# A hybrid sequence block on one core: half 0's convolution norm moved into half 1's state projection, and loads, squares and powers moved at the start of mixing

## The reference, cut to what matters

```python
h = rms_norm(x, g_pre_mix) * (1.0 + sc_m) + sh_m          # 2048 tokens x 1024
z = h @ w_in                                              # value, gate, ssm: 3 x 512 channels
a_out = conv_module(z_val * sigmoid(z_gate), ...)         # 31 taps per channel, layer norm, silu
b_out = s5_layer(z_ssm, ...)                              # complex linear recurrence, gelu, gated by its own projection
mixed = concatenate([rms_norm(a_out, g_out_conv), rms_norm(b_out, g_out_ssm)])
x = x + gt_m * rms_norm(mixed @ w_out, g_post_mix)
h = rms_norm(x, g_pre_ffn) * (1.0 + sc_f) + sh_f
y = moe_ffn(h, ...)                                       # sigmoid router, 8 of 64 experts, shared expert
x = x + gt_f * rms_norm(y, g_post_ffn)
```

## Time and profile before

| what | value |
|---|---|
| three runs | 2805.59, 2814.50, 2821.21 us; median 2814.5 us |
| the profiled execution | 2798.67 us, its span 2797.0 us |
| mean granted TensorE clock of the profiled execution | 0.958 of full speed |
| TensorE busy | 2543.7 us, 91% of the span |
| VectorE, ScalarE, GpSimd busy | 1552.1 us (55%), 1153.4 us (41%), 1384.4 us (49%) |

### The profile page before, as it was taken

The page is one execution under the profiler, slowest core; times in us unless marked ns, Lnnn a source line. Parts: engine busy times, 40 slices in busy tenths (PEclk is TensorE's granted clock), DMA queues, the critical chain, the costliest instruction groups (busy, mean ns, idle before and its releaser), DMA issues.

```text
span 2797.0 us, 49346 instructions
## 1 busy us (share of the span) xinstructions
PE 2543.7 (91%) x11232; PEld 1855.5 (66%) x11233; DVE 1552.1 (55%) x2764; ACT 1153.4 (41%) x1546; POOL 1384.4 (49%) x1726
## 2 busy tenths in 40 slices
PE   4999999957899998899999999999999999999990
PEld 1754664513456666688787877777887878777770
DVE  6379957993676776334333433444445544454535
ACT  5132313324233222344444444445555555555532
POOL 2011206013566665355555555565676677767662
PEclk7999999988899999999999999999999999999995
DMA  8152605454322322877777777788888988888978
GB/s 276 64 98 91 215 6 84 166 200 148 135 98 94 103 91 100 256 194 182 211 194 207 195 197 200 208 229 257 260 259 257 292 266 263 258 264 254 269 213 291
DMA packets 304953, 534.61 MB, mean 191 GB/s; under 512 B 38597, under 2 KB 204485, under 8 KB 304120
## 3 DMA queue, kind: packets, MB, share of 16 engines
q1 hardware_dynamic: 250248, 352.77, 38.0%
q0 software_dynamic: 51472, 173.70, 25.9%
q10 hardware_dynamic: 3168, 7.34, 0.7%
HBM read 395.75 MB, written 138.00 MB: 191 GB/s over the span
## 4 chain that ended last, share of the span: by engine, by line
PE 39%; issue 16%; POOL 8%; POOLq 6%; DVE 2%; DMA 1%; ACT 0%; SPq 0%; another core or an unknown queue 0%; ACTq 0%; DVEq 0%
PE psm L1122 29%; PE psm L1068 5%; PE psm L1115 3%; POOL arena L2265 2%; POOL arena L2262 2%; POOL st L2255 2%; POOLq L2261 1%; POOLq L2283 1%; POOLq L2274 1%; POOLq L2282 1%; POOL arena L2275 1%; PE psm L1090 1%; PE psm L1144 1%; POOL acc_d L2279 1%; DVE arena L2108 1%
## 5 line engine op out<-in xcount | busy, mean ns | idle before, releaser
L1122 PE MATMUL psm<-whi,xhi 128*128 (+1 forms) x1424 | 575.6, 404 | 42.5 <-issue 31.6
L1122 PE MATMUL psm<-whi,xlo 128*128 (+1 forms) x1424 | 559.4, 393 | 0.0
L1122 PE MATMUL psm<-wlo,xhi 128*128 (+1 forms) x1424 | 558.5, 392 | 0.0
L2009 DVE TENSOR_TENSOR arena<-psm,arena 128x256 f32<-128x256 f32 x178 | 75.5, 424 | 618.0 <-ACT arena L1504 612.7
L1122 PEld LDWEIGHTS psm<-whi,xhi 128*128 128x128 f32 x1424 | 269.5, 189 | 115.6 <-issue 65.0
L2270 POOL TENSOR_TENSOR wlo<-raw,whi (+1 forms) x64 | 331.0, 5172 | 20.3 <-ACT whi L1536 20.3
L1504 ACT ACTIVATE arena<-psm 128x256 f32<-128x256 f32 x178 | 68.2, 383 | 588.4 <-PE psm L1122 588.4
L1122 PE MATMUL psm<-whi,hhi 128*128 (+1 forms) x712 | 295.9, 416 | 14.3 <-POOL wlo L2270 7.0
L1122 PEld LDWEIGHTS psm<-whi,xlo 128*128 128x128 f32 x1424 | 269.2, 189 | 57.6
L2279 POOL DMA_INDIRECT acc_d<-arena x162 | 276.8, 1709 | 57.7 <-issue 53.7
L1122 PEld LDWEIGHTS psm<-wlo,xhi 128*128 128x128 f32 x1424 | 269.8, 189 | 50.9
(11 more groups left out here) (379 smaller groups left out, 4016.4 us busy)
## 6 DMA issues: line engine op xcount, KB each, us to landing
raw<-in_we_gate_dram SPq DMA_DIRECT2D x64, 1024.0 KB
raw<-in_we_up_dram SPq DMA_DIRECT2D x64, 1024.0 KB
raw<-in_we_down_dram SPq DMA_DIRECT2D x64, 1024.0 KB
arena<-in_w_ada_dram SPq DMA_DIRECT2D x12, 2048.0 KB
arena<-in_x_dram SPq DMA_DIRECT2D x32, 512.0 KB, 5.4
h_d<-arena SPq DMA_DIRECT2D x17, 512.0 KB, 2.7
arena<-in_w_in_dram SPq DMA_DIRECT2D x16, 512.0 KB, 6.2
mix_d<-bo SPq DMA_DIRECT2D x32, 256.0 KB, 2.3
```

The lines of the kernel that those rows point to most:

```text
L1122: m = TE.matmul(o, a, w, start=(n == 0), stop=(n == len(todo) - 1))
```

## The change

Five edits. Half 0's norm turns 0 to 3 are moved on TensorE, ScalarE and GpSimd behind the last four steps of half 1's `z_ssm` (`NORM_ZS` = 4), turns 4 and 5 to the products `V` of state groups 0 and 1 (`NORM_ZC` = 6), and turns 6 to 9 stay behind `zc` units 0 to 3; `tpk` and `sgk` follow. VectorE takes statistics 0 to 3 ahead of `states(1)`, and 4 to 7 among its groups. In SyncE's queue half 1's loads of the convolution weights q = 2 and of the Toeplitz table (`load_toe`) go behind six of the norm's stores, and q = 3 behind all eight. Four of the seven row loads go up into the stretch behind the last modulation weights; the router bias goes behind the last stores. `squares_joined(0)` and `ssn(0)` stand ahead of the products of the rows, and `rr(0)` ahead of GpSimd's index tables.

```diff
             if h == 0:
                 tpk += [("hT", 0, g, k) for g, k in UNITS]
+            for i in range(NORM_ZS if h else 0):
+                tpk += [("LF", 0, i)]
+                tpk += [("LB", 0, i - 2)] if i >= 2 else []
             tpk += [("UT", h, n) for n in range(8)]
...
+            sgk += [("ln", 0, i - 2) for i in range(2, NORM_ZC if h else 0)]
             for u, (q, b, w) in enumerate(ZC_UNITS):
                 sgk += [("zc", h, q, b)] if w else []
-                sgk += [("ln", 0, u - 2)] if h == 1 and 2 <= u < TPH + 2 else []
+                sgk += [("ln", 0, u + NORM_ZC - 2)] if h and u + NORM_ZC < TPH + 2 else []
...
             load_wz_conv(1, 1)
-            load_toe(1)
-            load_wz_conv(1, 2)
             for i in range(6):
                 store_bo(("ln", 0, i))
-            load_wz_conv(1, 3)
+            load_wz_conv(1, 2)
+            load_toe(1)
             for i in range(6, TPH):
                 store_bo(("ln", 0, i))
+            load_wz_conv(1, 3)
...
                 store_mod(n - 4)
+            for o in (s_mod_out0, s_mod_out1):
+                sp.wait_ge(o, 32)
+            sp.wait_ge(s_h2z_out, 32)
+            for dst, src in ((row[0], mod_d[2]), (rtmp[:, 0], A["g_post_mix"][0]), (rtmp[:, 1], A["g_pre_ffn"][0]),
+                             (rtmp[:, 2], A["g_post_ffn"][0])):
+                SY.dma_start(dst, src.partition_broadcast(P)).then_inc(s_row_in, 16)
...
-            for dst, src in ((row[0], mod_d[2]), (row[1], mod_d[4]), (row[2], mod_d[3]), (row[3], mod_d[5]),
-                             (rtmp[:, 0], A["g_post_mix"][0]), (rtmp[:, 1], A["g_pre_ffn"][0]), (rtmp[:, 2], A["g_post_ffn"][0])):
+            for dst, src in ((row[1], mod_d[4]), (row[2], mod_d[3]), (row[3], mod_d[5])):
                 SY.dma_start(dst, src.partition_broadcast(P)).then_inc(s_row_in, 16)
-            SY.dma_start(wr, A["w_router"][0].rearrange("(k p) e -> p k e", p=P)).then_inc(s_wr_in, 16)
-            SY.dma_start(rbias, A["b_router"][0].partition_broadcast(P)).then_inc(s_wr_in, 16)
             for i in range(3, 5):
                 store_bo(("ln", 1, i))
+            SY.dma_start(wr, A["w_router"][0].rearrange("(k p) e -> p k e", p=P)).then_inc(s_wr_in, 16)
...
@@ TensorE and ScalarE, z_ssm @@
+                    if h and j >= CH - NORM_ZS:
+                        norm_turn(0, j - (CH - NORM_ZS))
@@ TensorE, z_conv @@
                 for n in range(2):
                     input_state(h, n)
+                    if h:
+                        norm_turn(0, NORM_ZS + n)
...
-                    if h == 1 and u < TPH + 2:
-                        norm_turn(0, u)
+                    if h == 1 and u + NORM_ZC < TPH + 2:
+                        norm_turn(0, u + NORM_ZC)
@@ VectorE, states @@
                 if h:
+                    for k in range(NORM_ZS):
+                        norm_stats(k)
                     dve.wait_ge(s_tab_in, 32)
...
-                    if h and n >= 2:
-                        norm_stats(2 * n - 3)
+                    if h and n == 1:
+                        norm_stats(5)
...
-                    if h and 1 <= n <= 3:
-                        norm_stats(2 * n - 2)
-                if h:
-                    for k in range(5, TPH):
-                        norm_stats(k)
+                    if h and n < 3:
+                        norm_stats((4, 6, 7)[n])
@@ GpSimd, gate @@
+                for i in range(NORM_ZC if h else 0):
+                    norm_turn(0, i)
```

More of the change, by code:

```diff
@@ L59 @@
 NADA = 4
+NORM_ZS = 4
+NORM_ZC = 6
 EPS = 1e-6
@@ L369, in build @@
                 tpk += [("hT", 0, g, k) for g, k in UNITS]
+            for i in range(NORM_ZS if h else 0):
+                tpk += [("LF", 0, i)]
+                tpk += [("LB", 0, i - 2)] if i >= 2 else []
             tpk += [("UT", h, n) for n in range(8)]
-            if h == 1:
-                for i in range(TPH + 2):
-                    tpk += [("LF", 0, i)] if i < TPH else []
-                    tpk += [("LB", 0, i - 2)] if i >= 2 else []
+            for i in range(NORM_ZS, TPH + 2 if h else 0):
+                tpk += [("LF", 0, i)] if i < TPH else []
+                tpk += [("LB", 0, i - 2)] if i >= 2 else []
             if h == 0:
@@ L1085, in route @@
                 pe.wait_ge(s_ssn_ready, min(i + 2, NT))
+                if i == 0:
+                    pe.wait_ge(s_wr_in, 32)
                 if i:
@@ L1362, in z_conv @@
                     row_stats(2, xjunk)
+                for i in range(NORM_ZS, NORM_ZC if h else 0):
+                    norm_turn(0, i)
                 for u, (q, b, w) in enumerate(ZC_UNITS):
@@ L2040, in _ @@
             ssn(0)
+            dve.wait_ge(s_row_in, 7 * 16)
+            dve.wait_ge(s_dv_full, DVN["ada", 11] + 1)
+            do(tt(row[0], row[0], rtmp[:, 0], ALU.mult), stt(row[1], row[1], 1.0, rtmp[:, 1], ALU.add, ALU.mult),
+               tt(row[3], row[3], rtmp[:, 2], ALU.mult), V.memset(selcum[:, 0, :], 0.0), V.memset(ones64, 1.0))
+            V.tensor_copy(ndt[:, 3:4], ndt[:, 0:1]).then_inc(s_row_ready, 1)
             for i in range(NT):
@@ L2207, in _, with rr @@
                 norm_turn(1, i)
+            def rr(i):
+                c0 = 16 * (i % 2)
+                pool.wait_ge(s_ssn_ready, i + 1)
+                do(PO.tensor_tensor(st[:, c0 + 2:c0 + 3], st[:, c0:c0 + 1], mhalf[:, :], ALU.pow))
+                PO.tensor_tensor(st[:, c0 + 3:c0 + 4], st[:, c0 + 1:c0 + 2], mhalf[:, :], ALU.pow).then_inc(s_rr_ready, 1)
+            rr(0)
             pool.wait_ge(s_row_ready, 1)
```

18 lines of the change are left out of this document (4 added, 14 removed).

## The result

The changed kernel takes 2789.55 us (median of 20 runs, 2774.21 to 2807.64), the kernel before 2809.34 (20 runs beside it, 2793.08 to 2821.21). The ratio is 0.9937, 95% interval 0.9917 to 0.9958, a gain of 17.7 us (12 to 23); the two medians differ by 19.8, which lies in the same interval. The prediction was 2790 with a gain of 24.7: the direction and both places were right, both were sized too large. That the time itself was met is luck: over 20 runs the median before is 2809.3, and not the 2814.5 of the first three, from which the 24.7 were subtracted.

What follows compares the result with a forecast made beforehand. Bound taken: first `V`, states, statistics 4 to 7, convolution, then GpSimd's store wait ending half 1's norm. Gains 16.9 + 7.8 = 24.7 us took the 2814.5 median to 2789.8, rounded to 2790; range 2780 to 2806.

Steps and rivals of the forecast that it cites:

- both places: Half 0's norm, moved among projection steps and states: 16.9 us gain; start of mixing, at half 1's norm end: 7.8 us.
- The bound: Up to the convolution: first `V`, states, statistics 4 to 7, convolution; 17.8 us between states and convolution, mostly waiting for norm turns.
- First `V`: VectorE's first state operation moves from 396.41 to 400.0, behind added TensorE and ScalarE norm work: 3.6 us loss, bounds 1.8 and 6.
- The states: VectorE's state groups keep 59.0 us, GpSimd doing about the same beside them, some 18 us; bounds 54.5 and 62.
- The convolution: VectorE's convolution falls from 155.7 to 153.0 us as norm products leave its first quarter: gain 2.7, bounds 0 and 4.8.
- Second place: Start of mixing: earlier store of tile 3 lets GpSimd's product 5 start at 662.7, not 670.56; 7.8 us, bounds 0 and 10.9.
- the prediction's own sign: At the end of half 1's norm: the start-of-mixing forecast is wrong if GpSimd still waits for a store.
- 1: Before the convolution: gates of q = 0 replace the norm's statistics as the wait; convolution starts about 467, time 2798; chance 0.14.
- 5: Before `conv(1)`: the change does not do what it says; reduced to 1, with no chance of its own.
- 2: End of half 1's norm: store of tile 4 or 5 late behind `ws_raw` loads, only half 0's norm pays; 2798; chance 0.11.
- 3: SyncE's queue: moved row loads delay segment 8's store and half 1's norm turns; 2800 to 2810 us; chance 0.11.
- 4: TensorE becomes the bound, new waits at `UT` and turns 6 and 9 dropping its clock; 2835 us with 60 delay; chance 0.04.

Runs made afterwards that it cites:

- norm part alone: Only the diff's norm turns, statistics, `yn`, their stores and loads, against the kernel before; rows, first squares and powers unmoved: 2794.68 us, ratio 0.9943.
- rows late: Against the changed kernel, SyncE issues the store of half 1's output tile 3 ahead of the three row loads; no whole time or ratio given.
- `LB` 1 late: Against the changed kernel, second projection of half 0's tile 1, its ScalarE copy and sigmoid moved behind the eight `UT` transposes; ratio 0.9927 to the kernel before.

## Why the prediction was right, and where its sizes were off

**The bound.** Right: the convolution waited for half 0's statistics, and nothing took that wait's place. The norm part alone brings c 12.4 us nearer to z.

**First `V`.** 3.6 us of loss forecast, 1.8 on TensorE and 2.7 less 0.9 on ScalarE; 3.8 measured, of which `LB` 1 is 1.6 and TensorE's longer steps 2.2.

**The states: the mis-sized term.** "GpSimd does about the same beside them" and "I keep 59.0" failed: 62.4, so 3.4 us too few. Even the count was short (18 us of busy time; it is 25.24, since six norm products and two gates lie there, not four and one). And busy time was the wrong measure. A VectorE operation that reads from SBUF alone loses about 0.9 us (0.7 to 1.1 over these traces) to each GpSimd product of two SBUF tensors and 0.3 to 0.5 to a scaling, and one that reads PSUM loses nothing. By that rule on the timelines: four products before, eight after, 4 x 0.9 = 3.6 us, and one scaling fewer at 0.46; measured are 3.5.

The Trainium skill (SBUF — State Buffer, "SBUF: two separate sides") says that the pair of ports is locked by a VectorE operation "in a 2-port perf mode, or with two SBUF inputs (only against a GpSimd op that reads SBUF)" or by the GpSimd operation, and that the other one waits. I had used its lock for all busy time and set it aside for being twice the measured rate. Read with the condition on the operands it agrees with the traces: products fallen beside PSUM readers were free, and beside SBUF readers both sides lengthen (1.74 for 1.26 on GpSimd, 0.88 on VectorE). The passes with one tensor operand that lost too would come under its first clause; no run shows in which mode they ran. For the scaling the traces differ from it: 2.1 us long, it cost 0.3 to 0.5.

**The convolution.** 2.7 us of gain forecast, 2.0 measured. Before, 15 products and one scaling lay in it, after 14 products, which is 1.4 by the count. Added up over its instructions VectorE lost 14.4 us there before and 12.5 after. The rate of the earlier trace rows gave about the right size here because nearly all that GpSimd did there were products.

**Second place.** 7.8 us forecast, 4.25 measured. The forecast had product 5 at 33.8 us behind c; it started at 36.5. Of these 2.7 us, 1.4 are TensorE's slower start behind c in this profile; the forecast had assumed the rhythm of the kernel before: 3.64 us for sixteen matmuls that took 2.98, and 4.53 for eight (644.97) that took 3.60, so that product 5's sigmoid ended 35.0 us behind c and not 33.6. It also made the store's issue 1.1 late. The other 1.3 are the store: it took 7.9 us, not the 5.1 worked out from the loads' mean rate. That this term failed, the store's landing behind three row loads, doesn't hang on one profile: in all seven kernels that issue the store directly behind three row loads product 5 started 7.9 to 8.3 us behind its issue, also where TensorE's start was quick. Product 6 added 1.0, lengthened by a row product of VectorE, which I had costed as hidden ("run while TensorE works"). The same pair, with GpSimd as the one that waits. The kernel with rows late took out both, and its profile had the quick start that the forecast assumed: c to M became 40.6, against 40.8 forecast. By the prediction's own sign ("in the second if GpSimd still waits for a store") this place was half wrong: the wait is 1.70 us, and 3.2 to 3.4 in four other profiles with this order.

**The sum.** 16.9 became 12.5 and 7.8 became 4.25, together 16.8 of 24.7; z to J shows 17.0 and the ratio 17.7 (12 to 23). Two slips in the recorded sums move nothing: by the lock the sum would have been 27.5, not 27.6, and half of 1.07 is 0.54, not 0.58.

**Rivals.** 1 and 5: the gates were 6.1 us early. 2: products 6 and 7 were not held by stores in the changed kernel. 3: the four row loads were issued from 614.9 to 616.6, ahead of c; half 1's first norm turns follow each other at 4.66 us as before (they start 1.0 later behind c, which is TensorE's clock). 4: the granted clock in the convolution was 0.95, before 0.88.

## What to carry to other kernels

When work on GpSimd is moved beside VectorE, count its operations with two SBUF tensors against VectorE's operations that read from SBUF alone, and price each pair by one measured portion (0.9 us for 128x512 here), not by busy time; where VectorE reads PSUM they are free, so the place of a product inside a group is worth as much as its number. A store that frees a buffer goes out ahead of broadcast loads that nobody waits for yet: by bytes and a mean rate its landing is forecast too early. In a kernel whose executions spread by 1%, read a change as distances between two fixed instructions, take TensorE's start behind an idle time out of the comparison (here by the distance to the first product behind it), and let the medians confirm the sum.

## What the runs showed of the hardware that was not expected

The loss of VectorE comes in portions: eight scans of 128x128 take 3.12 us alone, 4.00 beside one GpSimd product and 4.85 beside two. Where GpSimd starts second, it pays: its product took 2.29 us for 1.27 beside a VectorE operation of 128x1024 (1.22 us) that had started 0.05 us before it. A scaling of 128x512 by GpSimd with one tensor and two values for each partition took 2.09 beside PSUM readers and 3.03 beside scans, which lost only 0.3. A store behind three broadcast loads in one queue let its product start 7.9 to 8.3 us after its issue, in seven kernels; without them directly in front it was 5.8 in the kernel before and with the norm part alone, and at most 6.0 with rows late. Behind idle times of 9 to 34 us the granted TensorE clock of the next 6 us lay between 0.50 and 0.74, in no order with the length of the idle time (0.73 behind 32.0 us; 0.56 behind 18.29 in the change and 0.71 behind 18.30 with `LB` 1 late), and this alone moved the norm of half 1 by up to 4 us.
